# Where a chunked recurrence's scan turns two of its operands: three groups of eight transposes moved between levels

## What is computed

```python
def wkv_scan(r, w, k, v, kk, a, s0, reverse):
    def step(s, inp):
        r_t, w_t, k_t, v_t, kk_t, a_t = inp
        sa = jnp.einsum('bhij,bhj->bhi', s, -kk_t)
        s = (s * w_t[:, :, None, :] + sa[..., None] * (kk_t * a_t)[:, :, None, :]
             + v_t[..., None] * k_t[:, :, None, :])
        return s, jnp.einsum('bhij,bhj->bhi', s, r_t)
...
def rwkv_mix(streams, s0, ln_w, ln_b, r_k, g_up):
    ...
    yf, sf = wkv_scan(r, wf, kf, v, kk, af, s0[0], False)
    yb, sb = wkv_scan(r, wb, kb, v, kk, ab, s0[1], True)
    y = yf + yb
    # group norm of each head, bonus term, gate
```

## Time and profile before

| what | value |
|---|---|
| median of 3 runs | 2904.25 us (2904.25 to 2905.07) |
| the profiled execution's own time | 2902.43 us |
| its span in the profile | 2900.5 us |
| TensorE busy (matmuls), share of the span | 2828.7 us, 98% |
| weight loads | 2393.2 us, 83% |
| VectorE / ScalarE / GpSimd | 1864.6 us (64%) / 1356.4 us (47%) / 251.0 us (9%) |
| mean granted TensorE clock | 0.996 of full speed |

### The profile page before, as it was taken

How to read it: one execution, slowest core, us unless ns; L and a number is a source line. 1 busy time by engine, 2 the same in 40 slices (tenths; PEclk the granted TensorE clock), 3 DMA queues, 4 the chain that set the end, 5 groups by cost and what they waited for, 6 DMA issues and landing times.

```text
span 2900.5 us, 56865 instructions
## 1 busy us (share of the span) xinstructions
PE 2828.7 (98%) x24171; PEld 2393.2 (83%) x24171; DVE 1864.6 (64%) x2553; ACT 1356.4 (47%) x1963; POOL 251.0 (9%) x303
## 2 busy tenths in 40 slices
PE   6999999999999999999999999999999999999998
PEld 2687888888888878888888888888888888888887
DVE  3597876777777776664445556799875555554444
ACT  3222446566665444444444444566544444444443
POOL 1000002333422000000000000133100000000000
PEclk8999999999999999999999999999999999999999
DMA  9997880000000668875665656666556666666564
GB/s 386 366 380 253 283 268 29 8 8 13 8 8 20 214 201 260 261 247 184 189 191 176 202 190 209 190 183 180 174 183 192 187 192 186 191 189 202 186 193 160
DMA packets 470782, 532.31 MB, mean 184 GB/s; under 512 B 22920, under 2 KB 422722, under 8 KB 469634
## 3 DMA queue, kind: packets, MB, share of 16 engines
q1 hardware_dynamic: 464754, 516.13, 55.4%
q0 software_dynamic: 3408, 10.42, 1.1%
q10 hardware_dynamic: 2368, 2.11, 0.3%
HBM read 522.29 MB, written 4.19 MB: 182 GB/s over the span
## 4 chain that ended last, share of the span: by engine, by line
PE 91%; DVE 4%; DMA 2%; ACT 1%; issue 1%; SPq 0%; DVEq 0%; ACTq 0%
PE ps L2468 14%; PE ps L2479 14%; PE ps L2481 14%; PE ps L2480 14%; PE ps L2644 11%; PE ps L2469 7%; PE ps L2971 4%; PE ps L2972 2%; PE ps L2490 2%; PE ps L2492 2%; PE ps L2491 2%; DMA raw<-in_w_mod 1%; PE ps L2654 1%; PE ps L2652 1%; PE ps L2540 1%
## 5 line engine op out<-in xcount | busy, mean ns | idle before, releaser
L1580 DVE TENSOR_TENSOR lo<-raw,hi 128x1024 fp32r<-128x1024 f32 x776 | 948.4, 1228 | 708.7 <-ACT hi L1063 703.7
L1063 ACT ACTIVATE hi<-raw 128x1024 fp32r<-128x1024 f32 x776 | 820.1, 1059 | 1067.8 <-PE ps L2481 602.0
L2479 PE MATMUL ps<-hi,mov 128*128 128x512 f32 x1408 | 553.2, 393 | 3.6 <-DVE mov L1648 3.6
L2481 PE MATMUL ps<-hi,mov 128*128 128x512 f32 x1408 | 549.0, 390 | 0.0
L2480 PE MATMUL ps<-lo,mov 128*128 128x512 f32 x1408 | 548.6, 390 | 0.0
L2479 PEld LDWEIGHTS ps<-hi,mov 128*128 128x128 f32 x1408 | 264.8, 188 | 58.4 <-issue 4.4
L2481 PEld LDWEIGHTS ps<-hi,mov 128*128 128x128 f32 x1408 | 264.6, 188 | 55.8
L2480 PEld LDWEIGHTS ps<-lo,mov 128*128 128x128 f32 x1408 | 264.9, 188 | 53.8
L2468 PE MATMUL ps<-mov,hi 128*128 128x512 f32 x864 | 305.7, 398 | 0.4 <-DVE mov L2398 0.3
L2468 PE MATMUL ps<-hid,hi 128*128 128x512 f32 x704 | 244.3, 394 | 0.0
L2469 PE MATMUL ps<-mov,lo 128*128 128x256 f32 x864 | 242.3, 280 | 0.0
(11 more groups left out here) (439 smaller groups left out, 4279.7 us busy)
## 6 DMA issues: line engine op xcount, KB each, us to landing
raw<-in_w_in SPq DMA_DIRECT2D x184, 512.0 KB, 4.8
raw<-in_w_gate SPq DMA_DIRECT2D x176, 256.0 KB, 2.9
raw<-in_w_up SPq DMA_DIRECT2D x176, 256.0 KB, 3.2
raw<-in_w_down SPq DMA_DIRECT2D x88, 512.0 KB, 3.4
raw<-in_w_ffn_gate SPq DMA_DIRECT2D x176, 256.0 KB, 2.9
raw<-in_w_ffn_up SPq DMA_DIRECT2D x176, 256.0 KB, 3.1
raw<-in_w_ffn_down SPq DMA_DIRECT2D x88, 512.0 KB, 4.5
raw<-in_w_out SPq DMA_DIRECT2D x64, 512.0 KB, 4.5
```

The lines of the kernel that those rows point to most:

```text
L1063: act.activation(hi[:, s, :, :], src, ACT.Copy).then_inc(hi_ready, 1)
L1580: dve.tensor_tensor(lo[:, s, :, :], raw_at(ph, i, j)[0], hi[:, s, :, :].bitcast(F32), ALU.subtract)\
L2479: pe.matmul(out, x(k)[:, 0, tokens], w_hi, start=first, stop=False)
L2481: mm = pe.matmul(out, x(k)[:, 1, tokens], w_hi, start=False, stop=last)
```

## The change

Three groups are placed elsewhere, with their copies on ScalarE; no arithmetic is added or removed.

- The forward keys' transposes (level 3) go wholly behind `T3`. Their wait for `oMV` goes there too.
- The backward removal rates (`tA` of direction 1) leave the first row and take the place in level 4, in the upper half of bank 5. Their copy `oA` leaves the head of ScalarE's unit and goes behind the two `Yb5` of level 5.
- The backward keys leave level 4 for level 5, which had no such group, and go to the upper half of bank 7 (`KEYS_AT`), behind a wait for `oMV` of direction 1. Their copy `oK` goes behind the front's activation of level 5 and, in norm units, behind `gate_out`, directly ahead of the two `Z` copies.
- `Z` of direction 1 now waits for `oA` of direction 1 instead of `oMV`.

```diff
-    KEYS_AT = (3, 5)
+    KEYS_AT = (3, 7)
...
             def unit(b, q, ahead=True, norm=None):
+                def keys(d):
+                    scan_pe[d].wait(act, (q, "tK"), b)
+                    scan_act[d].done(act.activation(tokK[d][:, :, :], chunks_of(ps[:, KEYS_AT[d], T:2 * T]), ACT.Copy), (q, "oK"))
+
...
-                    for name, src, bank, dst in (("oA", "tA", 0, tokR[d][:, :, 0, :]), ("oB", "tB", 1, tokBQ[d][:, :, 0:C])):
+                    for name, src, bank, dst in (("oA", "tA", 0, tokR[d][:, :, 0, :]), ("oB", "tB", 1, tokBQ[d][:, :, 0:C]))[d:]:
...
-                    for d in range(2 if l == 5 else 0):
-                        scan_pe[d].wait(act, (q, "tK"), b)
-                        scan_act[d].done(act.activation(tokK[d][:, :, :], chunks_of(ps[:, KEYS_AT[d], T:2 * T]), ACT.Copy), (q, "oK"))
+                    if l == 5:
+                        scan_pe[1].wait(act, (q, "tA"), b)
+                        scan_act[1].done(act.activation(tokR[1][:, :, 0, :], chunks_of(ps[:, 5, T:2 * T]), ACT.Copy), (q, "oA"))
+                        keys(0)
...
                     if norm is not None and l != 4:
                         group_norm(norm, l)
+                keys(1)
...
-                if l in (3, 4):
-                    d = l - 3
-                    if 0 in chunks and d == 0:
-                        scan_act[0].wait(pe, (q, "oMV"), b)
-                    if 0 in chunks and d == 1 and ahead:
+                if l in (3, 5):
+                    d = (l - 3) // 2
+                    if 0 in chunks:
+                        scan_act[d].wait(pe, (q, "oMV"), b)
+                    each(scan_pe[d], 0, (q, "tK") if last else None, KEYS_AT[d], lambda c, hs: stK[q][d][hs, c, :], None, off=T, chunks=chunks)
+                if l == 4:
+                    if 0 in chunks and ahead:
                         n, p = following(b, q)
                         front_act.wait(pe, (p, "sa1"), n)
-                    each(scan_pe[d], 0, (q, "tK") if last else None, KEYS_AT[d], lambda c, hs: stK[q][d][hs, c, :], None, off=T, chunks=chunks)
+                    each(scan_pe[1], 0, (q, "tA") if last else None, 5, lambda c, hs: stA[q][1][hs, c, 0:C], None, off=T, chunks=chunks)
...
-                    each(scan_pe[d], d, (q, "tA"), 0, lambda c, hs: stA[q][d][hs, c, 0:C], None)
+                    if d == 0:
+                        each(scan_pe[0], 0, (q, "tA"), 0, lambda c, hs: stA[q][0][hs, c, 0:C], None)
...
-                    between(b, q, l, ahead, range(0, 1))
+                    between(b, q, l, ahead, range(0, l != 3))
...
-                    between(b, q, l, ahead, range(1, NC))
+                    between(b, q, l, ahead, range(l != 3, NC))
...
-                    scan_act[d].wait(pe, (q, "oMV"), b)
+                    scan_act[d].wait(pe, (q, "oA" if d else "oMV"), b)
```

More of the change, by code:

```diff
@@ L495, in pe_names @@
     def pe_names(q, d):
-        out = (["tV"] if d == 0 else []) + ["tA", "tB"]
+        out = ["tV", "tA", "tB"] if d == 0 else ["tB"]
         for l in range(1, LEVELS):
-            out += [f"Y{l}", f"T{l}"] + (["MV"] if l == 1 + d else []) + (["tK"] if l == 3 + d else [])
+            out += [f"Y{l}", f"T{l}"] + (["MV"] if l == 1 + d else []) + (["tA"] if l == 4 and d else []) + (["tK"] if l == 3 + 2 * d else [])
         return out + ["Z", "A", "B"] + (["Y"] if q else []) + [f"st{n}" for n in range(1 - q, NC)]
     def act_names(q, d):
-        return ["U"] + (["oV"] if d == 0 else []) + ["oA", "oB", "Yb1", "Yb2", "Yb3", "oMV", "Yb4", "Yb5", "oK", "Z"]
+        return ["U"] + (["oV", "oA"] if d == 0 else []) + ["oB", "Yb1", "Yb2", "Yb3", "oMV", "Yb4", "Yb5"] + (["oA"] if d else []) + ["oK", "Z"]
     def dve_names(q, d):
```

## The result

| | before | changed |
|---|---|---|
| median | 2904.25 us | 2888.78 us |
| lowest to highest of 4 runs each | 2903.04 to 2905.07 us | 2887.22 to 2889.36 us |
| the profiled execution | 2902.43 us, span 2900.5 us | 2887.22 us, span 2885.2 us |

The changed kernel is 15.5 us faster, a ratio of 0.9945 with a 95% interval of 0.9931 to 0.996.

What follows compares the result with a forecast made beforehand. TensorE was taken as the bound, matmuls busy for 98% of the span. The terms, 11.0 + 3.1 - 0.8 - 2.6 = 10.7 us gained, take the 2904.25 us median to 2893.5 us; range of 8 in 10: 2887.5 to 2900.5 us.

Steps and rivals of the forecast that it cites:

- Level 3: Scan, 16 units: T3 no longer behind the wait for `oMV`, Y3 to Y4 from 3.33 to 2.64 us; 11.0 us saved.
- First row: Unit's first row, one group fewer: `rates` starts 0.39 us earlier, 3.1 us gained in 8 units; 0 in 7 norm units.
- The sigmoids follow `rates` and would move with it: First row: the prediction's argument against the rival that the shorter row gives nothing; no size of its own.
- The first rival: First row gives nothing, `rates` held by copies or the 8 units by VectorE: 3.1 us less, 2896.6 us; chance 0.15.
- Level 4: Level 4 of each unit: one group of transposes replaces another with the same wait for `sa1`; 0.
- Level 5: T5 to Z, twelve records added: 0.8 us lost in 9 units without a norm, 2.6 us in 7 norm units.
- ScalarE takes over level 3: Rival, level 3: T3 waits for both Yb3 copies or Yb4 is late; 0.25 us per unit, 2900.5 us; chance 0.14.
- The last copy of the keys holds the Z copies: Rival, end of level 5: `oK` of direction 1 delays Z copies, 17.4 us lost, 6.4 us slower, 2910.7 us; chance 0.07.
- the best end: Whole change, all bounds at their best: 13.0 + 4.0 + 2.7, 19.7 us faster.

Runs made afterwards that it cites:

- the context units put back: Changed kernel, but context (norm) units keep backward removal rates in the first row and backward keys in level 4, level 5 empty: 2885.35 us, ratio 0.9939.
- the two added copies: Changed kernel with two more ScalarE copies that nothing waits for, behind `oMV` of direction 1 in level 3: 2888.98 us, ratio 0.9955.

## Why the prediction was right, and where it was off

**Level 3, 0.69 us by 16: right.** The level's step fell by 0.72 us in norm units and 0.74 in x units, in the change and alone. Y3 to T3 is 1.16 us as read from levels 4 and 5; T3 to Y4 came at 1.45 us and not 1.48.

**First row, 0.39 us in the 8 units with `rates` and no norm: the place right, the term too large.** The row itself is shorter by 0.39 us in all of them, and `rates` starts 1.60 us behind the first transpose, as forecast. The norm units hand it back in full to VectorE, as forecast (Y1-Y2 +0.39, confirmed by the context units put back). Not foreseen was that six of the 7 x units hand half of it back too, +0.07 us in Y1-Y2 and +0.11 in Y2-Y3; unit (0, 1) keeps all of it. "The sigmoids follow `rates` and would move with it" was true, but behind them VectorE's own instructions met GpSimd's masks at another moment and took longer (below). The term is 0.21 us in 6 units and 0.38 to 0.39 in two, 2.0 us instead of 3.1. The first rival was thus partly true.

**Level 4: right**, 0 in both kinds of unit.

**Level 5: right.** Norm units lost 0.35 us (forecast 0.37), x units 0.06 (forecast 0.09), the first and the last unit 0.13 to 0.15. The twelve records cost 29 ns each. The 31 ns of the prediction were read a little too high: in the earlier trace rows the 64 transposes start 29 ns apart, the last one 1.84 us behind the first, and the rest of the 1.99 us is the step from there to `rates`. The 25 ns of the Trainium skill's page "TensorE: Matmul & The Clock Gate", section "Wait — 56ns, not 53.3ns?", were not reached.

**ScalarE takes over level 3: refuted**, by 0.25 us of idle time before Yb4 and by the two added copies. **The last copy of the keys holds the Z copies: refuted.** The Z copy of a norm unit waits 0.37 us for TensorE, with the copy ahead of it, where the earlier trace rows has 0.65.

**The sum.** By the corrected terms the steps give 11.7 + 2.0 - 2.5 - 0.7 = 10.5 us. The unit sums give 11.4; of the difference, 0.3 us are hundredths in the steps behind Z of the x units (11.12 to 11.08 us each), the rest is rounding and steps of the first and the last unit that had no term. Forecast: 10.7. The mechanism was right to within a microsecond. As forecast, level 3 is the whole of it: the other two moves stand in the forecast with 3.1 - 0.8 - 2.6 = 0.3 us lost, and by whole units they gave nothing.

**What the sum did not hold** is the pauses. The median fell by 15.5 us, some 4 us more than the steps give. In the profiled executions before lost 8 us in pauses, of which 6 on TensorE and 1.8 on VectorE, and the changed kernel about 1. The step that was missing is in the first part of the prediction: the 22.7 us without a matmul were read as waits with a cause each, and a pause that belongs to no wait was named only as something that might grow. The repetition of before (2.5 us less) and its shift by 128 instructions (3.5 us less with 1.9 us of work added) speak for pauses that belong to position and execution, not to the steps; the shift of the changed kernel, which brought none, says that position is not all. Shown is that the two kernels differ in them; why the changed one stays free of them, shifted too, is open.

**The range held by luck.** Its lower end was to be half of the distance from 2893.5 us to the best end. The best end is 2904.25 - 19.7 = 2884.5 us, so that half is 2889.0 and not 2887.5, and the measured 2888.78 us would have been 0.2 us outside. What carried it so low is the pauses, for which the prediction has no term.

**Behind the scan** the forecast had nothing given back. Between the end of the scan and the end of the span the first profiles have 1967.0 us before and 1969.8 changed, but the other executions lie between 1967.9 and 1970.5 without order by edit. About half of the difference is the clock. The last matmuls ahead of TensorE's longest wait behind the scan, before and then changed:

```profile
1028.74 1.13 PE L2521 MATMUL ps<-nt,basics 128*128 128x256 f32 x4 [1.24 <-DVE nt L2116]
...
1010.75 2.08 PE L2527 MATMUL ps<-nt,basics 128*128 128x256 f32 x4 [1.24 <-DVE nt L2122]
```

In the changed kernel the granted clock was 0.50 in this stretch and 1.00 in that of before, which costs it 0.95 us. Windows where the feed-forward starts (columns of the earlier trace rows; the seventh figure behind the window, PEclk, is the granted clock), before:

```profile
1032.00:1036.00 4.00, 2.48 (x6) 2.02 (x7) 4.00 (x11) 2.83 (x6) 0.00 (x0) 0.64 0.20 69
1036.00:1040.00 4.00, 4.00 (x17) 3.27 (x17) 4.00 (x11) 2.55 (x5) 0.00 (x0) 0.93 0.00 0
```

and changed:

```profile
1016.00:1020.00 4.00, 3.52 (x8) 2.81 (x9) 4.00 (x11) 2.60 (x7) 0.00 (x0) 0.50 0.00 0
1020.00:1024.00 4.00, 4.00 (x17) 3.26 (x16) 4.00 (x11) 2.88 (x6) 0.00 (x0) 0.92 0.01 4
```

In both kernels TensorE stands for 3.65 us there, waiting for VectorE, until 1033.52 and 1016.48 us, and comes out of it at the lower level of 1.2 GHz (0.50). The granted clock stays there for 3.0 us of work before and for 4.2 changed, which is another 0.55 us by the matmuls' starts. The whole stretch at 0.50 was 3.4 us in the first profile of before, 10.3 in that of the changed kernel, and 6.8 to 10.3 in all the others, before's second and its shifted one among them: it goes with the execution, not with the edit.

## What to carry to other kernels

Filler between two steps of a chain is free while another engine's copy sets the gap, but only filler that waits for nothing: a wait that stands in an in-order queue ahead of ready work costs its full length, and moving four instructions past it was worth 11.7 us here, while moving two whole groups to other levels was worth nothing. Before counting a shorter stretch as a gain, look whose queue sets the next step, in each kind of iteration apart: here 7 of 15 took all of it back and 6 more took half. And where single executions differ by 2 to 3 us in pauses, compare like steps where no pause falls, and run the old kernel again and shifted, before crediting an edit with what the median shows.

## What the runs showed of the hardware

**Pauses without a wait.** In the kernel before, TensorE's stream stops for 0.2 to 1.1 us at places where the profile shows nothing that it waits for; the pauses recur mostly at the same instructions in another execution of the same program (4 of 6 us) and stand elsewhere when 128 instructions are put ahead. In the changed kernel they come to about 0.4 us or less in a whole scan, with and without such a shift. The Trainium skill's page "Runtime: NRT & Kernel Launch", section "Instruction fetch mechanics", says that an engine's instructions are fetched ahead in blocks at a cost that is mostly hidden. No run here shows the fetch, so whether these pauses are its unhidden part stays open.

**VectorE and GpSimd take turns.** In norm units VectorE's pair of scans takes 1.76 us in some executions and 2.36 in others. Before, unit (2, 0), then unit (1, 0), each with the masks of L968:

```profile
580.39 0.69 DVE L1902 TENSOR_TENSOR_SCAN dirs<-kscan,dirs 128x260 f32<-128x260 f32 x1
580.40 1.21 POOL L968 TENSOR_TENSOR lev<-U,kscan 128x256 f32<-128x256 f32 x1
...
519.99 1.28 DVE L1902 TENSOR_TENSOR_SCAN dirs<-kscan,dirs 128x260 f32<-128x260 f32 x1
519.99 1.80 POOL L968 TENSOR_TENSOR lev<-U,kscan 128x256 f32<-128x256 f32 x2
```

Where the scan starts first (by 4 ns in the trace), it takes 0.69 us and the mask 1.21; where the mask starts first (by 2 ns), the scan takes 1.28 us and this mask, the first of the two in the last row, 0.72. A mask with no such neighbour takes 0.72 to 0.73 us. So one of the two stands while the other works, and less than a hundredth of a microsecond decides 0.6. The same is seen in x units: the changed kernel's scans take 2.30 us where before has 1.90 in most, and the product of L1886 (L1880 before) 1.18 us instead of 0.77, each beside a mask. The Trainium skill's page "SBUF — State Buffer", section "SBUF: two separate sides", gives this rule: the two engines share a pair of ports, and an instruction of VectorE with two inputs from SBUF and one of GpSimd that reads SBUF exclude each other, the first to start going first; these rows agree. It was read from rows; no run varied the masks.

**A copy's price.** On ScalarE a 128x256 copy that has another behind it has a row of 0.38 to 0.40 us but moves the queue by 0.27 us; a budget of covers made from the rows' durations overstates it by half.
